# A two-block layer on one Trainium2 core: the mixers' order, the place of the weights' DMAs, and the start

## What is computed

```
first block:
  shift, scale, gate = split(silu(c) @ ada_w + ada_b, 3)
  h    = rmsnorm(x, norm_pre) * (1 + scale) + shift
  proj = h @ w_in                        # 3072 columns, for three mixers
  attention (8 heads, window 128, ALiBi slopes, sinks)  * silu(...)
  RWKV-7 (4 heads, delta rule, decay)                   * silu(...)
  gated linear attention (4 heads, chunks)              * silu(...)
  x1   = x + gate * rmsnorm(concat(all three) @ w_out, norm_post)
second block:
  h    = rmsnorm(x1, norm_g)
  proj = h @ w_in_2                      # q, k, v, qi, ki, wi, z_a, u, z_b, gates
  index scores select 256 keys for each query (at most)
  a    = attention over the selected keys * silu(z_a)    # rotary q, k
  b    = pooled means of u, mixed by group * silu(z_b)
  out  = x1 + (g0 * (a @ w_branch_a) + g1 * (b @ w_branch_b)) @ w_out_2
```

## Time and profile before

| | us |
|---|---|
| median of 3 runs | 4033.17 (4031.93 to 4033.19) |
| the profiled execution | 4033.76 |
| its span | 4032.0 |
| PE busy | 3704.3 (92%) |
| DVE, ACT, POOL busy | 1840.7, 1583.7, 447.6 |

### The profile page before, as it was taken

How to read it: one execution, slowest core, us unless ns; L and a number is a source line. 1 busy time by engine, 2 the same in 40 slices (tenths; PEclk the granted TensorE clock), 3 DMA queues, 4 the chain that set the end, 5 groups by cost and what they waited for, 6 DMA issues and landing times. The chain is left out here.

```text
span 4032.0 us, 69389 instructions
## 1 busy us (share of the span) xinstructions
PE 3704.3 (92%) x28412; PEld 2794.4 (69%) x28412; DVE 1840.7 (46%) x4514; ACT 1583.7 (39%) x3575; POOL 447.6 (11%) x695
## 2 busy tenths in 40 slices
PE   4999999976999999959989999999996999999998
PEld 4788888855666666627767777778784666666676
DVE  4111111125666666613467677766565333333322
ACT  1222222223333333311466655777772333433320
POOL 0000000004444444310000000000000000000000
PEclk9999999997999999979999999999998999999999
DMA  8111111122111111142111112412214111111111
GB/s 271 49 48 48 48 48 48 48 96 101 63 68 68 68 68 68 45 134 73 45 47 46 46 46 83 133 53 65 73 44 167 64 54 43 57 46 43 62 63 55
DMA packets 137765, 282.16 MB, mean 70 GB/s; under 512 B 35064, under 2 KB 84104, under 8 KB 130960
## 3 DMA queue, kind: packets, MB, share of 16 engines
q1 hardware_dynamic: 114624, 261.76, 18.6%
q10 hardware_dynamic: 20560, 8.16, 0.8%
q0 software_dynamic: 2304, 8.39, 0.5%
HBM read 181.80 MB, written 96.47 MB: 69 GB/s over the span
## 5 line engine op out<-in xcount | busy, mean ns | idle before, releaser
L2376 ACT ACTIVATE at_pT<-at_bank 128x512 f32<-128x512 f32 (+3 forms) x320 | 154.9, 531 | 615.0 <-PE at_bank L2268 613.7
L270 PEld LDWEIGHTS p_bank<-p_hT,w_in 128*128 128x128 f32 x3328 | 375.4, 192 | 7.7 <-issue 7.7
L270 PE MATMUL p_bank<-p_hT,w_in 128*128 128x128 f32 x3328 | 376.8, 274 | 0.0
L1759 PEld LDWEIGHTS p_bank<-p_hT,w_in_rest 128*128 128x128 f32 x3072 | 352.6, 195 | 31.2 <-issue 17.0
L1759 PE MATMUL p_bank<-p_hT,w_in_rest 128*128 128x128 f32 x3072 | 359.0, 279 | 11.8 <-DVE p_st L2057 11.7
L2394 DVE CUSTOM_DVE_ANT_0 at_s<-at_bank,at_bias 128x512 f32<-128x512 f32 (+3 forms) x320 | 182.8, 609 | 388.1 <-PE at_bank L2255 382.5
L276 PE MATMUL p_bank<-w_in,p_hT 128*128 128x512 f32 (+2 forms) x1024 | 311.6, 462 | 0.0
L1879 ACT ACTIVATE p_r<-p_acc,p_mid 128x384 f32<-128x384 f32 (+13 forms) x224 | 292.6, 1306 | 30.6 <-DVE p_acc L2084 26.4
L1750 PE MATMUL p_bank<-arena,p_hT 128*128 128x512 f32 x512 | 232.0, 606 | 37.2 <-ACT p_hT L1873 28.6
L988 PE MATMUL b_banks<-b_wout,b_yT 128*128 128x512 f32 x512 | 262.4, 645 | 2.8 <-DVE b_r L1397 1.5
L276 PEld LDWEIGHTS p_bank<-w_in,p_hT 128*128 128x128 f32 x1024 | 172.5, 191 | 124.6 <-issue 118.9
(11 more groups left out here) (400 smaller groups left out, 5789.7 us busy)
## 6 DMA issues: line engine op xcount, KB each, us to landing
stage<-p_st SPq DMA_DIRECT2D x16, 1856.0 KB, 6.8
arena<-stage SPq DMA_DIRECT2D x16, 1856.0 KB, 8.2
at_rest<-stage SPq DMA_DIRECT2D x16, 1280.0 KB, 5.9
stage<-p_pr SPq DMA_DIRECT2D x128, 128.0 KB, 1.8
p_ada<-in_ada_w SPq DMA_DIRECT2D x6, 2048.0 KB, 13.5
p_xt<-in_x SPq DMA_DIRECT2D x16, 512.0 KB, 7.4
b_x<-in_x SPq DMA_DIRECT2D x16, 512.0 KB, 3.3
x<-b_x SPq DMA_DIRECT2D x16, 512.0 KB, 2.7
```

Source lines behind the costliest of these rows:

```text
L270: last = mm(out, w_in[:, k, c:c + P], hT[:, k, 1:P + 1], start=(k == 0), stop=(k == KD - 1))
L1759: last = mm(bank[:, m * P:(m + 1) * P], weights(k, c + m * P, c + (m + 1) * P), hTs[:, n % 2, k, :], start=(k == 0), stop=(k == KD - 1))
```

## The change

- Stage one: four chunks of `ada_w` in four buffers (two of them are columns of `w_in` that are loaded later), so that `fetch_ada` waits from the fifth on only; two sums in turn (even and odd blocks), which PE adds up with twice as many products; Exp ahead of ACT's loads; the first x's norm and h ahead of Sin, and the rotary angles behind the first `take_h`. The q weights wait for all four chunks. The second x goes out behind them and ahead of the rest of the weights, and x of tile n + 2 in turn n.
- Stage two: new orders on all four engines. `attend` makes four products of 512 columns with the values as weights, channels on partitions; ACT copies them (`take_attended`), PE transposes them back (`turn_attended`). `join` is cut in X and Y. At p = 15 SP also loads the first tile of x1. `rwkv_out` now waits for both halves of SA.
- Stage three: the weights' and small loads on SP (z_a in plain order, two DMAs), `g_ch` at the very start of the program; ACT's `take_h(0)` follows `scale_x(0)`. The early operands are waited for where they are used. Stage four: `fetch_za`, four DMAs for a tile.

The diff's core:

```diff
-                    if c >= 2:
-                        sp.wait_ge(S["chunk_used"], c - 1)
-                    sp.dma_start(ada[:, c % 2, :, :], ada_src[:, :, c * 512:(c + 1) * 512]).then_inc(S[f"ada_loaded{c}"], 16)
+                    if c >= 4:
+                        sp.wait_ge(S["chunk_used"], c - 3)
+                    sp.dma_start(ada_chunk[c], ada_src[:, :, c * 512:(c + 1) * 512]).then_inc(S[f"ada_loaded{c}"], 16)
...
                 fetch_weights("gv", (C_GV, IN1))
+                sp.wait_ge(S["chunk_used"], 4)
                 for k in range(KD):
                     for g in range(A_KV):
                         sp.dma_start(w_in[:, k, 0:512].rearrange("p (c g d) -> p g c d", g=2, d=HEAD)[:, g],
                                      wsrc[:, k, 256 * g:256 * g + 256].rearrange("p (c d) -> p c d", d=HEAD)).then_inc(S["q_weights"], 16)
+                sp.wait_ge(S["xn_ready"], 1)
+                sp.dma_start(xt[:, :], A["x"][0][P:2 * P, :]).then_inc(S["x_loaded"], 16)
...
-                    if tile.more:
-                        sp.wait_ge(S["xn_ready"], n)
-                        sp.dma_start(xt[:, :], A["x"][0][bass.ds(n * P, P), :]).then_inc(S["x_loaded"], 16)
+                    if not isinstance(i, int):
+                        sp.wait_ge(S["xn_ready"], n + 1)
+                        sp.dma_start(xt[:, :], A["x"][0][bass.ds((n + 1) * P, P), :]).then_inc(S["x_loaded"], 16)
...
-                        last = mm(B[6][:, 4 * c + m:4 * c + m + 1], acc[:, c % 2, m * P:(m + 1) * P], ones[:, 0:1], start=True, stop=True)
+                        for e in range(2):
+                            last = mm(B[6][:, 4 * c + m:4 * c + m + 1], acc[:, c % 2, e, m * P:(m + 1) * P], ones[:, 0:1], start=(e == 0), stop=(e == 1))
                     last.then_inc(S["summed"], 1)
...
+                act.wait_ge(S["c_loaded"], 16)
+                f(ce[:, :], cc[:, :], ACT.Exp, scale=-1.0).then_inc(S["exp_done"], 1)
                 load = lambda dst, src: act.dma_start(dst, src).then_inc(S["weights_loaded"], 16)
...
-                act.wait_ge(S["c_loaded"], 16)
-                f(ce[:, :], cc[:, :], ACT.Exp, scale=-1.0).then_inc(S["exp_done"], 1)
+                norm_x(1, 0)
+                act.wait_ge(S["scale_ready"], 1)
+                take_h(1, hTs[:, 0])
                 act.wait_ge(S["reduced"], 1)
                 for which in range(2):
                     f(tables[:, :, which, :], red[:, which, :, :], ACT.Sin)
-                norm_x(1, 0)
-                act.wait_ge(S["scale_ready"], 1)
-                take_h(1, hTs[:, 0])
...
-                    part = acc[:, c % 2, :]
-                    ch.link(ts(part, ada[:, c % 2, 0, :], ca[:, 0:1], None, ALU.mult))
-                    for k in range(1, KD):
-                        last = stt(part, ada[:, c % 2, k, :], ca[:, k:k + 1], part, ALU.mult, ALU.add)
-                        if k < KD - 1:
-                            ch.link(last)
-                    last.then_inc(S["chunk_used"], 1)
+                    parts, block = acc[:, c % 2], ada_chunk[c]
+                    for k in range(KD):
+                        part = parts[:, k % 2, :]
+                        if k >= 2:
+                            dve.wait_ge(S["block_added"], KD * c + k - 1)
+                        if k < 2:
+                            last = ts(part, block[:, k, :], ca[:, k:k + 1], None, ALU.mult)
+                        else:
+                            last = stt(part, block[:, k, :], ca[:, k:k + 1], part, ALU.mult, ALU.add)
+                        last.then_inc(S["block_added"], 1)
+                    dve.wait_ge(S["block_added"], KD * (c + 1))
+                    dve.sem_inc(S["chunk_used"], 1)
...
-                rotary_angles(dve, ch, v, S, pos_i, pos, freq, ang, turns, red)
                 for c in range(4):
...
                 take_h(1, hTs[:, 0]).then_inc(S["hT_dve"], 1)
+                rotary_angles(dve, ch, v, S, pos_i, pos, freq, ang, turns, red)
...
+                        sp.dma_start(arena[:, HEAD_COLUMNS:HEAD_COLUMNS + D], x1[rows_of(0), :]).then_inc(x_early, 16)
...
                 def rwkv_out(n):
+                    pe.wait_ge(S["sa_ready"], 2 * n + 2)
...
                 def attend(n):
                     for j in range(4):
                         pe.wait_ge(S[f"prob{j}_taken"], n + 1)
+                    bank = bank_for("attT", n)
+                    for half in range(0 if n else 1, 2):
+                        for g in range(2):
+                            value = Staged(n - 1 + half).v
+                            last = mm(bank[half_of(g), :], value[:, HEAD * g:HEAD * g + HEAD], pT[:, g::2, half::2, :], start=(half == 0 or n == 0), stop=(half == 1))
+                    last.then_inc(S["attT_done"], 1)
+
+                def turn_attended(n):
+                    pe.wait_ge(S["attT_taken"], n + 1)
                     bank = bank_for("att", n)
-                    for h in range(A_HEADS):
-                        j, e, g = h // 4 + 2 * (h % 4 // 2), h % 2, h // 4
-                        for half in range(0 if n else 1, 2):
-                            value = Staged(n - 1 + half).v
-                            last = mm(bank[:, h * HEAD:(h + 1) * HEAD], pT[:, j, 2 * e + half, :], value[:, HEAD * g:HEAD * g + HEAD], start=(half == 0 or n == 0), stop=(half == 1))
+                    for i in range(4):
+                        last = tr(bank[:, i * P:(i + 1) * P], flat(s[:, 0:2, :])[:, i * P:(i + 1) * P], ident[:, :])
...
+                def take_attended(n):
+                    act.wait_ge(S["attT_done"], n + 1)
+                    f(flat(s[:, 0:2, :]), bank_of("attT", n), ACT.Copy).then_inc(S["attT_taken"], 1)
...
+                def fetch_weights(name, c, e):
+                    for k in range(0, KD, KD // 2):
+                        sp.dma_start(weights(slice(k, k + KD // 2), c, e), wsrc[:, k:k + KD // 2, c:e]).then_inc(S[f"{name}_weights"], 16)
+
+                fetch_weights("ki", C2_KI, C2_ZA)
+                fetch_weights("za", C2_ZA, C2_U)
+                load = lambda dst, src: sp.dma_start(dst, src).then_inc(S["early_loaded"], 16)
+                load(early["qk_g"][:, 0:8, :], A["q_norm_g_2"].unsqueeze(1).broadcast_to([P, 8, HEAD]))
+                load(early["qk_g"][:, 8:10, :], A["k_norm_g_2"].unsqueeze(1).broadcast_to([P, 2, HEAD]))
+                load(early["allowed"][:, :], A["k_allowed"])
+                load(early["halves"][:, :], row(A["k_halves"]))
+                load(early["pscale"][:, :], A["pool_scale_2_ch"])
+                load(early["pw"][:, :, :], A["pool_w_2"][0].rearrange("g c d -> c g d"))
                 store_h(0)
+                fetch_weights("u", C2_U, C2_ZB)
+                fetch_weights("zb", C2_ZB, C2_GATES)
+                sp.dma_start(early["mb"][:, :], A["merge_bias_2"][0].rearrange("b (m p) -> p (b m)", p=P), allow_slow_non_contiguous=True).then_inc(S["mb_loaded"], 16)
                 stored = indexed = fetched = 0
                 for kind, n, s in PLAN:
...
-                    act.wait_ge(S["x_loaded"], 16 * (n + 1))
+                    act.wait_ge(S["x_loaded"] if n else x_early, 16 * max(n, 1))
...
-                load = lambda dst, src: act.dma_start(dst, src).then_inc(S["early_loaded"], 16)
-                load(early["g_ch"][:, :], A["norm_g_2_ch"])
...
-                for k in range(KD):
-                    for g in range(A2_KV):
-                        act.dma_start(weights(k, C2_ZA, C2_U).rearrange("p (c g d) -> p g c d", g=2, d=HEAD)[:, g],
-                                      wsrc[:, k, C2_ZA + 256 * g:C2_ZA + 256 * g + 256].rearrange("p (c d) -> p c d", d=HEAD)).then_inc(S["za_weights"], 16)
-                fetch_weights("u", C2_U, C2_ZB)
-                fetch_weights("zb", C2_ZB, C2_GATES)
-                act.wait_ge(S["early_loaded"], N_WEIGHTS)
                 take_h(0)
...
+                        if n == 0:
+                            dve.wait_ge(S["early_loaded"], N_WEIGHTS)
+                            ch.link(ts(qk_g[:, 8:10, :], qk_g[:, 8:10, :], -1.0, None, ALU.mult))
                         rest_of_qk(n)
...
+                def fetch_za(n):
+                    for g in range(A2_KV):
+                        for e in range(2):
+                            dst = za[64 * g:64 * g + 64, :].rearrange("p (c e t) -> p e c t", e=2, t=P)[:, e]
+                            src = stage[ORDER[n] * P + 64 * e:ORDER[n] * P + 64 * e + 64, T_ZA + 256 * g:T_ZA + 256 * g + 256]
+                            load("za_loaded", dst, src.rearrange("p (c t) -> p c t", t=P))
```

347 lines of the change are left out of this document (182 added, 165 removed).

## The result

The changed kernel takes 3897.94 us (3894.62 to 3899.92 over four runs) against 4032.55 before (4025.88 to 4033.19): a ratio of 0.9669, 95% interval 0.9652 to 0.9686. The forecast was 3914, so the change brought 16 us more than its sum said. The profiled execution took 3894.62 us.

A forecast was written before the change was run, and what follows sets the result against it. PE was taken as the limiting engine throughout, so its waits mattered. Mixers -82, boundary -28.6, start -3.5, second x -6.6 and additions +1.6 gave -119 from 4033.76, so 3914 us; range 3892 to 3948.

The forecast's parts named there:

- (1): Mixers: the second state_products stands behind more PE work, next_state is done 2 us ahead, so the 2.1 us wait goes.
- (2): Mixers: other work now precedes the first gla round, so the score reductions end about 1 us before it.
- step (3): Mixers: the second gla round no longer needs att_taken; attT, the ring's user before it, is copied on ACT in 0.6 us.
- The floor of 44.4: Mixers: length in us of a steady tile-pair period if PE never waits, its work having fallen by 1.5.
- seven margins of 0 to 0.7: Mixers: seven places in the new order with 0 to 0.7 us to spare; 1.2 us a period left for them.
- The slow patch: Mixers: slower PE work following the 2 us wait for the state in most periods, 1.4 us a period, expected to go.
- at nothing: Boundary to stage three: cost given to later sync-queue loads, u and z_b behind store_h(0), and to z_a's extra issues.
- rival B: Start is later: setup ends at 38 or more, +4 us, 3918 to 3920; sign: first product after 60 us; chance 0.35.
- 4 us later: Start: with Exp first, ACT's loads go out 4 us later than before, and their landing sets the end of POOL's setup.
- A: Rival, mixers: the new order trades its waits for others, period 48.5 us, time 3951; chance 0.17.
- C: Rival, mixers: POOL's gate makes PE wait at turn_y, each microsecond over 0.7 costing 15; slower than before; chance 0.03.
- D: Rival, boundary: late q weights (arena_loaded) undo the gain there, time 3943; chance 0.02.

The follow-up runs named there:

- e5: Changed kernel with attend alone as before (16 products of 64 columns), VectorE's reading of it moved ahead of its second state step: 3923.69 us.
- e8: Changed kernel with four small copies added on ACT ahead of take_Z(3) in each period: 3900.11 us.
- e6: Changed kernel with the first gla round put back right behind the second scores: 3946.28 us.
- e7: Changed kernel with three powers added on GpSimd right ahead of the rwkv gate in each period: 3950.66 us.
- e9: The changed kernel run once more, unaltered, as a yardstick: 3898.16 us.
- e12: Changed kernel with TensorE's sums ahead of the setup wait, setup loads behind c's chunks, and stage three's second x loaded from ACT: 3881.33 us.
- e3: Changed kernel with TensorE summing c's first two chunks ahead of its wait for GpSimd's setup: 3887.74 us.
- e4: Changed kernel with the nine setup loads moved from ACT's queue to the sync queue, ahead of c's first chunk: 3886.24 us.
- e11: Changed kernel with two powers added on GpSimd right ahead of the rwkv gate in each period: 3914.67 us.
- e10: Changed kernel with sums ahead of the setup wait, setup loads behind c's chunks, stage three's second x load ahead of h's store: 3887.29 us.

## Why the prediction was right, and where it was off

**The mixers: mechanism right, one term too big.** Steps (1) and (2) hold with their margins: in the changed trace the second `state_products` starts at 1098.64 and `next_state` ended at 1096.50 (2.1 us; forecast 2), the first gla round starts at 1090.12 and the reductions ended at 1088.8 (1.3; forecast 1). In step (3) the second round starts at 1108.34, the copy of `attT` ended at 1107.36 (1.0); e5 shows that VectorE's early reading frees it too. The floor of 44.4 is 44.63. The term that failed is the 1.2 us a period "left for" seven margins of 0 to 0.7: it measured 0. They are small (0.7 ahead of `grams`, 0.5 ahead of `rwkv_out` and of XY(3), 1.0 ahead of `attend`, 1.4 ahead of the transposes of y) and all above nothing, and a margin above nothing costs nothing, in any period, since the periods are alike. e8 puts a microsecond more on ACT ahead of one of them without a cost. Over thirteen periods that is 16 us too little gain, nearly the whole miss; the floor's 0.2 takes 3 back, the period forecast at 41 was 37.7, and the one ahead of it, which I held for unchanged, lost 2.1.

**The slow patch** comes behind its wait, as the forecast had it: e6 and e7 bring both back, though not in every period (ten and nine of twelve). Its price there is 1.6 us, 1.4 in the sum.

**The boundary** came out at -28.9 for -28.6. But "at nothing" was wrong for what follows on the sync queue. I asked what u and z_b cost when they go out behind `store_h(0)`, and not what else is in that step: it also fetches the second x. In the profiled run that wait is 1.83 us without a slow patch; in e9 it is 2.99 with one, and from its first product to the end the two runs differ by 3.5 us, 2.9 of them in the first tile. e12 takes nearly all of the wait away.

**The start** went by rival B: the setup ended at 38.6, not at the 34 that I took as the middle, and the chain behind it took 21.1 us for my 22, so 59.68 for 56. That profile lies inside the bounds; the seven others with this stage one have the setup at 39.1 to 40.1 and the first product at 60.2 to 61.1, just past the bound of 60 that I gave as B's sign. I had two bounds and no row between them; the middle of two mechanisms is neither.

The step that failed is "4 us later". The third and the ninth of ACT's loads, before and after:

```profile
4.12 1.21 ACTq L354 DMA_DIRECT2D p_mu_w<-in_rwkv_mu_w_ch  x1
...
10.99 0.61 ACTq L354 DMA_DIRECT2D p_wa<-in_rwkv_a  x1
```

```profile
21.72 0.61 ACTq L363 DMA_DIRECT2D p_wa<-in_rwkv_a  x1
```

The first load goes out 1.9 us later (4.86 for 3.01), the ninth 10.7 us later, since the third issue takes 7.43 us for 1.21 and the two for gk take 6.48 for 3.72. From its issue to its landing the ninth takes 11.4 us for 9.8. Nor did the landing set the setup before: there GpSimd began right behind the first x's length, at 30.26, with the ninth load landed at about 21. Now it waits 5.19 us for it.

The Trainium skill, "DMA: Bandwidth & Descriptors", section on queues, rings and completion order, has the engines take the queues in turn. The upper bound, T0 = 38 with loads that end only with c's stream, is close to what the traces show: in e3, where both are waited for as they land, GpSimd has the last load at 34.06 and VectorE the fourth chunk at 34.26. That turns are the reason is not shown. e4 shows the reverse: the same loads ahead of the chunks on one queue, and the setup is over at 28.8.

**The second x of stage one** gave 7.5 for 6.6, since the slow clock behind it cost 2.0 and not 1.1. **The small additions:** the doubled last sums are there (3.60 us for 1.88), but PE waits for the mixers' rows behind them until 30.4 us after stage one's last product in both kernels, so they cost nothing.

**The rivals.** A and C need a steady period above 46; none was. e7 and e11 give C's price: its point of decision is 1.4 us and not 0.7, beyond it 0.83 us cost 0.86 in each period, and 1.91 us cost 3.5 where the slow patch joins and 2.0 where it does not. D did not occur.

## What to carry to other kernels

Lay the order out by hand and look at each margin's sign: in a loop whose periods are alike a positive margin is worth all of its wait, here with margins down to 0.5 us, and what is to be feared is the wait that brings the low clock behind it. When a step moves in a queue, list every instruction in it and ask of each who waits for its end; here the one left out (a load of half a megabyte) was the only new wait. An engine that waits for everything at its start can hold up a stage through work that needs almost none of it: one wait moved was worth 10 us.

## What was not expected of the hardware

**Small loads can hold up a queue while the DMA engines are nearly idle.** The strip of DMA use in the changed kernel from 1660 to 1690, in 40 slices of 0.75 us:

```profile
DMA  0028878999999610000000111125999999999999
GB/s 0 0 25 309 150 120 268 401 352 369 396 407 404 198 57 19 22 21 22 21 16 23 39 34 26 44 53 146 289 339 386 410 380 410 404 404 407 401 393 396
...
early_qk_g<-in_q_norm_g SPq DMA_DIRECT2D x1, 256.0 KB, 16.6
...
early_pscale<-in_pool_scale_ch SPq DMA_DIRECT2D x1, 2.0 KB, 12.8
```

For some 9 us the engines move 16 to 57 GB/s, where they reach 410, while the store of h and behind it the second x, u and z_b stand behind six loads of 2 to 256 KB; one of 2 KB takes 12.8 us. In e12 such a stretch lies under the x that came from another queue. Whether these loads come to rest on one engine, as the small share of busy engines might suggest, is not shown; putting them behind the x and the weights was not tried.

**VectorE slows beside GpSimd.** Six scalar_tensor_tensor of 128x512 take 4.06 us with GpSimd idle (e10) and 5.85 with its tensor_tensor beside the first half of them (e3); the two multiplications ahead of them take 2.53 for 0.88. In e4 the same operations take 5.06 and 2.29 us under the second chunk, with GpSimd's beside them. The Trainium skill, "GPSIMD Engine Reference", section 1, lists the SBUF interfaces as shared with VectorE, with contention for its instructions in a 2-port perf mode or with two inputs in SBUF. The six operations have two such inputs, and the trace agrees for them; whether the multiplications, with one, run in such a mode, no run here shows.

**The low clock does not go by the wait's length alone.** The same 1.91 us brought it in ten of twelve periods of e6 and nine of twelve of e7, and not in the others; before, the 2 us wait for the state brought it in ten of twelve. It also followed 1.71 (e10) and 2.99 us (e9), and neither 0.83 (e11) nor 1.83 us, at 1689.87 in the changed kernel's first profile. What else decides stays open.
